# A two-layer encoder trunk on one core: Hyena pieces placed between the 24 gate and lift blocks of the attention branch, and 512-column products in the input and state-space stages

## Chip, core and metric

The kernel runs on one core of a Trainium2 chip (trn2). The metric is the device time in microseconds (us) of one execution. Engines: TensorE (PE, with its weight loads as PEld), VectorE (DVE), ScalarE (ACT), GpSimd (POOL) and SyncE (SP), which only issues DMAs. TensorE's clock has two levels, 1.2 and 2.4 GHz; a granted clock of 1.00 in a view is 2.4 GHz.

## The reference

Two layers, each of which projects the stream x (256 tokens, 2048 features), runs three mixers of width 1024 on it, lifts each mixer's output to 2048 features, gates and adds the three, and normalises. Cut to what matters:

```python
proj = x @ w_in[i]                       # inputs of the mixers, gate logits, ple logits
y_a = s5_mixer(a_x, ...) * silu(a_z)     # state space, per 16-channel group
filt_f = hyena_filters(L, ...)           # MLP -> taps (256, 2 dirs, 2 orders * 1024), rfft
y_b = hyena_mixer(b_u, ..., filt_f, ...) * silu(b_z)
y_c = mla_mixer(c_q, c_kv, c_kr, ...) * silu(c_z)
lifted = einsum('blnc,ncd->blnd', stack([y_a, y_b, y_c]), w_lift[i])
mixed = sum(sigmoid(gate_logits) * lifted, axis=branch) @ w_out[i]
x = layer_norm(ALPHA * x + mixed + ple)
# hyena_filters: h = sin-MLP(feats) @ w3 + b3; h *= decay; both directions joined;
#                divided by sum |h|; rfft
# hyena_mixer:   v, x1, x2 = split(short_conv3(u)); z = v
#                for n, gate in ((0, x1), (1, x2)):   # the two orders
#                    conv = irfft(rfft(z) * filt_f[:, n]); z = gate * (conv + bias[n] * z)
```

## The kernel before, in words

**Blocks.** The large weights come as 184 blocks per layer of 128x2048 float32, in halves of 128x1024, through a ring of four slots that SyncE fills in a fixed order. 170 of them are split into two parts: ACT copies a quarter (128x512) into WH in fp32r (L359, `make_wh`), DVE subtracts to get WL (L373, and L364 in the state-space loop; `make_wl`). WH and WL hold one block, in quarters of their own: a quarter of the next block can be written when PE has used that quarter of the current one (`parts_used`). The stream is split the same way into XH and XL. A tile product then takes three matmuls of 256 columns, `WH*XH`, `WH*XL`, `WL*XH` (L1354, `half_block`), so a block of 16 tiles takes 48.

**Stages of a layer**, in PE's order: `ax` (8 blocks, the S5 inputs, banks 0 and 1, evicted by ACT); `s5` (a loop of 8 turns, `ct`, with 8 blocks each, which project all else that is needed and whose results ACT evicts into PROJ, and between them the state-space work of one channel tile: `turn` L1390, `inputs` L1405, `lags` L1423, `outputs` L1440 and L1446); GLU and latent attention with unsplit weights (L1336, L1514); `lifta`, the 8 heads with the 24 gate and lift blocks of branch A between their parts; `filt`, the Hyena filters in four chunks of 512 channels (taps L1579 and L1580, their transform L1596, sums of absolute values L1603); `hy`, the two orders of the long convolution (transposes L1619, forward transform L1631, inverse L1639); `lift`, 24 blocks for branch B and 24 for branch C, in loops of 12; then `ple`, `out`, normalisation.

In `filt` and `hy` each step of PE is followed by one of DVE or ACT: DVE multiplies taps by DEC, which a POOL DMA brings (L874), forms ED and the sums (L884 to L889) and the short convolutions (L862 to L865); ACT takes absolute values and evicts (L1237 to L1248); DVE multiplies spectra (L920 to L928) and closes each order (L936 to L946). No weight block is used from the end of `lifta` to the first block of `lift`.

**What sets the order.** Each engine runs its own program in order; semaphores join them. `take_bank` waits until a PSUM bank has been read out, by counts that the table FILLS gives per stage.

Of the kernel before, what the change touches and what calls it, by code (L numbers as in the profile page):

```python
# [34 lines left out]
P = 128  # L35
# [59 lines left out]
STAGES = ["ax", "s5", "glu", "mla", "lifta", "filt", "hy", "lift", "ple", "out"]  # L95
# [83 lines left out]
def trunk(nc, x, blocks, lp, bc, w1, w2, b3, decay, feats, pT, pos, consts, out):  # L179
    with ExitStack() as ctx:  # L180
# [7 lines left out]
        XH, XL = sb("XH", DT * T, dt=F32R), sb("XL", DT * T, dt=F32R)  # L188
# [35 lines left out]
        xh, xl = split(XH[:], DT), split(XL[:], DT)  # L224
# [43 lines left out]
        HH, AB, ED, DEC, B3 = area(35, 8), area(121, 8), area(65, 8), area(25, 4), area(29, 2)  # L268
        FRE, FIM = area(89, 16), area(105, 16)
        ZT, YRE, YIM, TM = HH, ED, area(25, 8), AB  # L270
# [4 lines left out]
        YCH, YCL, YBH, YBL = parts("YCH", 89, 8), parts("YCL", 97, 8), parts("YBH", 105, 8), parts("YBL", 113, 8)  # L275
        MIXA = area(25, 16)
        MIX, PLE = area(73, 16), area(24, 16)
# [25 lines left out]
        b3_loaded, b3_cleared = sem("b3_loaded"), sem("b3_cleared")  # L303
        x_ready = sem("x_ready")
# [3 lines left out]
        us_written, us_landed, u4_loaded = sem("us_written"), sem("us_landed"), sem("u4_loaded")  # L308
        e_ready, bk_ready, bk_used = sem("e_ready"), sem("bk_ready"), sem("bk_used")
# [8 lines left out]
        sums_ready, sums_used = sem("sums_ready"), sem("sums_used")  # L318
        z_in, yf_ready, yb_ready = sem("z_in"), sem("yf_ready"), sem("yb_ready")
        mix_moved = sem("mix_moved")  # L320
# [15 lines left out]
        def split_number(layer, block_, turn=0, per=0):  # L336

            skipped = 0 if block_ <= B_LIFT0 else UNSPLIT[0] if block_ < B_W3 else UNSPLIT[1] if block_ <= B_OUT0 else UNSPLIT[2]
            return layer * SPLITS + (block_ - skipped + 1) + turn * per

# [55 lines left out]
        def _(pool):  # L396
# [5 lines left out]
            with pool.Fori(0, DEPTH) as layer:  # L402
# [32 lines left out]
                pool.wait_ge(mix_moved, layer + 1)  # L435
                for c in range(CHUNKS):
                    if c:

                        pool.wait_ge(psum_free[5], read_out(layer, "filt", 5, c - 1))
# [5 lines left out]
                    pool.dma_start(DEC, decay[c]).then_inc(b3_loaded, 16)  # L445
# [22 lines left out]
        def _(dve):  # L468
# [10 lines left out]
            with dve.Fori(0, DEPTH) as layer:  # L479
# [17 lines left out]

                make_wl(dve, v, layer, B_AX)
# [39 lines left out]
                st.did(v.reciprocal(S[1], S[0])); st.wait()  # L538
                make_wl(dve, v, layer, B_AX + 2)
# [12 lines left out]
                st.did(v.reciprocal(S[4], S[4])); st.wait()  # L552
                make_wl(dve, v, layer, B_AX + 3)
# [7 lines left out]
                st.did(v.tensor_tensor(S[6], S[6], S[4], ALU.mult)); st.wait()  # L561
                make_wl(dve, v, layer, B_AX + 4)
# [9 lines left out]
                st.did(v.tensor_tensor(lr[2], PA[:, 0:COLS], PB[:, 0:COLS], ALU.subtract)); st.wait()  # L572
                make_wl(dve, v, layer, B_AX + 5)
# [15 lines left out]
                product(square, powers(1, 2), powers(3, 2), 2, PA[:, 0:2 * COLS], PB[:, 0:2 * COLS])  # L589
                make_wl(dve, v, layer, B_AX + 6)  # L590
# [3 lines left out]
                product(factor, powers(0, 5), graw, 5, V[:, 0:5 * COLS], V[:, 2 * T:2 * T + 5 * COLS])  # L594
                make_wl(dve, v, layer, B_AX + 7)
# [18 lines left out]
                st.wait()  # L614
                make_wl(dve, v, layer, B_AX + 8)

                with dve.Fori(0, WT) as ct:
                    st.enter(ct, DVE_S5_STEPS)
                    wl_for = lambda j, q: make_wl_quarter(q, layer, B_S5 + j + 1, ct, 8)
# [44 lines left out]
                    wl_for(1, 1)  # L664
                    st.wait()
# [16 lines left out]
                    wl_for(2, 2)  # L682
                    st.did(v.tensor_tensor(terms(T2, 5), ci, g_r, ALU.mult))
# [6 lines left out]
                    wl_for(3, 2)  # L690
                    wl_for(3, 3)
# [9 lines left out]
                    wl_for(4, 1)  # L701
                    full(3, "s5", ct)
# [12 lines left out]
                    wl_for(5, 1)  # L715

# [14 lines left out]
                    wl_for(6, 1)  # L731
                    st.wait()
# [9 lines left out]
                    wl_for(7, 0)  # L742
                    st.did(v.tensor_tensor(split(V[:, 0:T], PAIRS), split(U4[:, bass.ds(ct * T, T)], PAIRS),
# [3 lines left out]
                    dve.wait_ge(y4_free, layer * WT + (ct + 1))  # L747
                    st.wait()
# [56 lines left out]
                for i in range(2):  # L805
# [6 lines left out]
                    round_phase(dve, st, *ARG, arg_ready)  # L812


                for h in range(HEADS):
# [23 lines left out]
                    if h < HEADS - 1:  # L839
                        make_wl(dve, v, layer, lift_a(3 * h + 3))  # L840
                    for b in range(2):
                        out_of(b, "lifta", h)
                        full(2 + b, "lifta", h)
                        free(v.tensor_tensor(split(MIXA, DT)[:, 2 * h + b, :], GA[:, b, :], bank[2 + b][:, 0:T], ALU.mult), 2 + b)
# [4 lines left out]
                dve.wait_ge(mix_moved, layer + 1)  # L849
                v.memset(B3, 0.0).then_inc(b3_cleared, 1)  # L850
# [4 lines left out]
                bct = tiles(BC, 0, 24)  # L855

                def short_conv(m):
                    u, o = PROJt[:, m, :], bct[:, m, :]
                    if m:

                        dve.wait_ge(z_in, layer * ZIN + m)
# [5 lines left out]


                hh = HH.rearrange("p (q c) -> p q c", q=4)
                for c in range(CHUNKS):  # L870
                    dve.wait_ge(b3_loaded, layer * (48 * CHUNKS) + (c + 1) * 48)
                    for q in range(4):
                        full(2 + q, "filt", c)
                        free(v.tensor_tensor(hh[:, q, :], bank[2 + q][:, :], DEC[:, (q % 2) * CW:(q % 2 + 1) * CW], ALU.mult), 2 + q)  # L874
                    for q in range(4):
                        out_of(2 + q, "filt", c)

                    v.memset(hh[0:1, 2, :], 0.0).then_inc(taps_ready, 1)
                    dve.wait_ge(taps_ready, layer * CHUNKS + (c + 1))
                    if c:  # L880

                        full(1, "filt", 2 * c - 1)
# [4 lines left out]
                    dve.wait_ge(abs_ready, layer * CHUNKS + (c + 1))  # L887
                    st.did(v.tensor_tensor(AB[:, 0:2 * CW], AB[:, 0:2 * CW], AB[:, 2 * CW:4 * CW], ALU.add)); st.wait()
                    v.tensor_tensor(AB[:, 0:CW], AB[:, 0:CW], AB[:, CW:2 * CW], ALU.add).then_inc(sums_ready, 1)  # L889
                    for m in range(6 * c, 6 * c + 6):  # L890
                        short_conv(m)
                    dve.wait_ge(ed_ready, layer * CHUNKS + (c + 1))
                dve.wait_ge(z_in, layer * ZIN + 24)
                full(6, "filt", 0)
                ns = NS
# [955 lines left out]
```

## Time and profile before

| | |
|---|---|
| median of 3 runs | 2981.0 us (2979.93 to 2981.59) |
| the profiled execution | 2978.65 us, of which 2977.0 us span |
| PE busy | 2751.8 us (92%), 20392 matmuls |
| DVE, ACT busy | 1846.7 us (62%), 1305.6 us (44%) |
| mean granted TensorE clock | 0.966 |

A busy time is the union of an engine's instructions; matmuls overlap each other, so their own durations add up to more than the time they take. The spacing of their starts is what one costs.

### The profile page before, as it was taken

The page shows a single profiled execution, that of the slowest core. Times are in us where ns is not written, and L with a number is a line of the kernel's source. Part 1 is how long each engine was busy: PE and PEld are TensorE (multiplying, and loading weights), DVE is VectorE, ACT ScalarE, POOL GpSimd, SP SyncE. Part 2 cuts the span into 40 slices and gives each one's busy share as a digit, 9 for nine tenths or more (in the row PEclk, how much of TensorE's full clock was granted, in tenths as well). Part 3 has the DMA queues.
Part 4 walks back from the last instruction along what each step waited for, and adds up shares of the span by engine and source line. Part 5 has one row for each costly group of instructions (what it writes and reads, how often), then busy time and mean ns, then how long its engine had stood idle before and what let it go on. Part 6 is the DMA issues. An engine that isn't in the chain of part 4 may idle for free.

```text
span 2977.0 us, 54930 instructions
## 1 busy us (share of the span) xinstructions
PE 2751.8 (92%) x20392; PEld 2570.1 (86%) x20392; DVE 1846.7 (62%) x3164; ACT 1305.6 (44%) x2319; POOL 109.1 (4%) x202
## 2 busy tenths in 40 slices
PE   6999999899977899999879999998999688999996
PEld 6999999779944799999779999997799447999986
DVE  6777767525567655565487777774355666555655
ACT  4455555525521244453335555555255212444532
POOL 1100000000000000000021000000000000000000
PEclk9999999899988999999989999999999889999999
DMA  6444444334421155555354444443344102555542
GB/s 226 151 146 144 144 144 141 103 128 157 149 64 36 68 180 181 183 177 171 106 177 148 147 142 148 138 145 102 136 149 142 57 29 86 180 183 180 178 165 92
DMA packets 115086, 411.08 MB, mean 138 GB/s; under 512 B 15300, under 2 KB 15322, under 8 KB 114448
## 3 DMA queue, kind: packets, MB, share of 16 engines
q1 hardware_dynamic: 106704, 390.12, 38.9%
q0 software_dynamic: 8256, 19.26, 2.1%
q8 instruction: 82, 1.34, 0.2%
q14 instruction: 44, 0.36, 0.0%
HBM read 403.02 MB, written 6.29 MB: 137 GB/s over the span
## 4 chain that ended last, share of the span: by engine, by line
PE 86%; DVE 7%; issue 3%; DMA 2%; ACT 2%; POOL 0%; DVEq 0%; PEldq 0%; POOLq 0%; ACTq 0%; PEld 0%; SPq 0%
PE bank L1354 64%; PE bank L1336 5%; PE bank L1446 2%; PE bank L1423 2%; PE bank L1405 2%; PE bank L1631 2%; PE bank L1639 1%; PE bank L1596 1%; PE bank L1390 1%; PE bank L1440 1%; PE bank L1514 1%; DMA ARENA<-in_decay 1%; PE bank L1579 1%; PE bank L1539 1%; PE bank L1538 1%
## 5 line engine op out<-in xcount | busy, mean ns | idle before, releaser
L359 ACT ACTIVATE WH<-ring 128x512 fp32r<-128x512 f32 x1360 | 856.4, 631 | 1107.1 <-PE bank L1354 982.3
L1354 PE MATMUL bank<-XH,WH 128*128 128x256 f32 x4160 | 1197.5, 288 | 75.2 <-DVE XL L501 44.6
L1354 PE MATMUL bank<-XL,WH 128*128 128x256 f32 x4160 | 1183.5, 284 | 0.0
L1354 PE MATMUL bank<-XH,WL 128*128 128x256 f32 x4160 | 1182.9, 284 | 0.0
L373 DVE TENSOR_TENSOR WL<-ring,WH 128x512 fp32r<-128x512 f32 x848 | 579.2, 691 | 512.8 <-ACT WH L359 507.9
L1354 PEld LDWEIGHTS bank<-XH,WH 128*128 128x128 f32 x4160 | 804.8, 193 | 84.9 <-DVE XL L501 45.0
L1354 PEld LDWEIGHTS bank<-XL,WH 128*128 128x128 f32 x4160 | 805.0, 194 | 0.1
L1354 PEld LDWEIGHTS bank<-XH,WL 128*128 128x128 f32 x4160 | 804.4, 193 | 0.0
L364 DVE TENSOR_TENSOR WL<-ring,WH 128x512 fp32r<-128x512 f32 x512 | 351.0, 688 | 192.3 <-ACT WH L359 186.2
L1336 PE MATMUL bank<-ARENA,ring 128*128 128x256 f32 x704 | 158.9, 388 | 20.2 <-ACT ARENA L1186 17.5
L1336 PEld LDWEIGHTS bank<-ARENA,ring 128*128 128x128 f32 x704 | 134.8, 194 | 43.6 <-issue 22.9
L1354 PE MATMUL bank<-MIXH,WH 128*128 128x256 f32 x512 | 144.5, 282 | 7.0 <-issue 5.5
L1354 PE MATMUL bank<-MIXL,WH 128*128 128x256 f32 x512 | 143.7, 281 | 0.0
L1354 PE MATMUL bank<-MIXH,WL 128*128 128x256 f32 x512 | 143.7, 281 | 0.0
L1354 PEld LDWEIGHTS bank<-MIXH,WH 128*128 128x128 f32 x512 | 96.5, 188 | 9.0 <-issue 6.7
L1354 PEld LDWEIGHTS bank<-MIXL,WH 128*128 128x128 f32 x512 | 96.5, 189 | 0.0
L1354 PEld LDWEIGHTS bank<-MIXH,WL 128*128 128x128 f32 x512 | 96.5, 188 | 0.0
L1639 PE MATMUL bank<-CON,ARENA 128*128 128x256 f32 x256 | 65.0, 421 | 19.3 <-DVE ARENA L928 19.3
L1639 PEld LDWEIGHTS bank<-CON,ARENA 128*128 128x128 f32 x256 | 54.4, 214 | 31.6 <-issue 22.6
L1354 PE MATMUL bank<-YAH,WH 128*128 128x256 f32 x256 | 75.0, 293 | 0.0
L1579 PE MATMUL bank<-ring,ARENA 64*128 64x512 f32 x64 | 27.3, 886 | 50.8 <-DMA ARENA<-in_decay 50.8
L1354 PE MATMUL bank<-YAH,WL 128*128 128x256 f32 x256 | 71.9, 281 | 0.0
(290 smaller groups left out, 3558.3 us busy)
## 6 DMA issues: line engine op xcount, KB each, us to landing
ring<-in_blocks SPq DMA_DIRECT2D x736, 512.0 KB, 3.3
ARENA<-in_bc POOLq DMA_DIRECT2D x2, 2048.0 KB, 8.4
ARENA<-in_decay POOLq DMA_DIRECT2D x8, 512.0 KB, 3.6
ARENA<-in_x SPq DMA_DIRECT2D x1, 2048.0 KB, 9.1
u_scratch<-ARENA POOLq DMA_DIRECT2D x16, 128.0 KB, 3.3
ARENA<-u_scratch POOLq DMA_DIRECT2D x64, 32.0 KB, 3.3
y_scratch<-ARENA POOLq DMA_DIRECT2D x16, 128.0 KB, 2.0
ARENA<-y_scratch POOLq DMA_DIRECT2D x64, 32.0 KB, 2.8
```

Of the source, the lines that this page charges most:

```text
L359: nc.scalar.activation(wh[q], raw(which[0], q), ACT.Copy).then_inc(wh_ready[q], 1)
L364: nc.vector.tensor_tensor(wl[q], raw(which[0], q), wh[q].bitcast(F32), ALU.subtract).then_inc(w_used[slot(which[0], q // 2)], 1)
L373: vec.tensor_tensor(wl[q], raw(which[0], q), wh[q].bitcast(F32), ALU.subtract).then_inc(w_used[slot(which[0], half)], 1)
L1336: ins = mm(o, w[:, (w0 + i) * P:(w0 + i + 1) * P], rhs(i), start=i == 0, stop=i == k - 1)
L1354: ins = mm(o, w_, x_, start=start and i == 0 and n == 0, stop=stop and i == 7 and n == 2)
L1390: ins = nc.tensor.transpose(bank[b][:, i * P:(i + 1) * P], part_of(E, i % 2, i // 2, q, P), ident)
L1405: ins = mm(o, ET[:, q % 2 * CW + i * P:q % 2 * CW + (i + 1) * P], u4(q), start=True, stop=True)
L1423: ins = mm(bank[4 + d][:, q * P:(q + 1) * P], b, f, start=(r == 0), stop=(r == 1))
L1446: ins = mm(o, f, x_, start=False, stop=(d == 1 and r == 1))
L1579: mm(bank[2 + q][:, :], H2[rows, t * P:(t + 1) * P], w[rows, c * CW:(c + 1) * CW], start=True, stop=False)
L1631: ins = mm(bank[b][:, :], tab[:, t, m * P:(m + 1) * P], ZT[:, t * W + half * CW:t * W + (half + 1) * CW], start=(t == 0), stop=(t == 1))
L1639: ins = mm(bank[c % 2][:, 0:T], yft[r][:, m, c * P:(c + 1) * P], (idft_sin if r else idft_cos)[:, m, :], start=(k == 0), stop=(k == 3))
```

## The change

**512-column products.** XH and XL become the two halves of one tensor XX. In `ax` and `s5` a tile product is two matmuls: WH against XH and XL together (512 columns, into columns 0 to 255 and 256 to 511 of one bank), and WL against XH (256 columns, onto the first half). ACT copies out the second half, then DVE adds the first half to it and frees the bank (`add_input`, `add_block`), at one place for each block in DVE's order. `lifta`, `lift`, `ple` and `out` keep three matmuls.

**Hyena pieces.** Stages `filt` and `hy` are gone. The 24 blocks of branch C come next after `lifta`, written out, as stage `hyc`; before block k PE does a piece of the Hyena work by its place s in the order (k = 12 o + s): s 0 and 3 taps, 2 and 5 filter transform, 6 transposes, 7 two quarters of the forward transform, 8 and 9 a quarter each (and in 8 the sums), 10 and 11 half of the inverse each. Filters are made per order o, in half the space. The pieces use banks 4 to 7. DVE does its pieces between the two halves of `make_wl` of block k + 1 and behind them. The w3 block is copied out of the ring by DVE, DEC has a semaphore of its own and shares memory with YIM, and the sum of branch A is written at its final place, so that the copy L848 goes. Branch B's 24 blocks follow, in the loop.

```diff
-    "filt": [8, 8, 4, 4, 4, 4, 1, 0],
-    "hy":   [8, 8, 4, 4, 4, 4, 4, 4],
-    "lift": [16, 16, 16, 16, 0, 0, 0, 0],
+    "hyc":  [8, 8, 8, 8, 18, 18, 20, 18],
+    "lift": [8, 8, 8, 8, 0, 0, 0, 0],
...
+                    if c == 0:
+                        pool.wait_ge(psum_full[5], nth(layer, "mla", 5, 8))
+                    elif c == 2:
+                        pool.wait_ge(psum_free[7], read_out(layer, "hyc", 7, hyc(0, "inv", 1)))
+                    pool.sem_inc(dec_free, 1)
+                    pool.dma_start(DEC, decay[c]).then_inc(dec_loaded, 16)
...
+                    def add_block(j):
+                        tile_ = PROJ[:, bass.ds(ct * (8 * T) + j * T, T)]
+                        dve.wait_ge(moved, layer * (9 * WT) + (ct * WT + (j + WT + 1)))
+                        free(v.tensor_tensor(tile_, tile_, bank[j % 2][:, 0:T], ALU.add), j % 2)
...
-                v.tensor_copy(MIX, MIXA).then_inc(mix_moved, 1)
...
+                for k in range(24):                                     # DVE
+                    o, s_ = k // 12, k % 12
+                    make_wl(dve, v, layer, B_LIFT + 24 + k + 1, halves=(0,))
+                    if s_ in (0, 3):
+                        taps_out(o, s_ // 3)
...
+                    if s_ in (7, 8, 9):
+                        if s_ == 8:
+                            full(6, "hyc", hyc(o, "sums", 0, 6))
+                            free(v.reciprocal(NS[:, o * 8:o * 8 + 8], bank[6][:, 0:8]), 6)
+                        product(o, (0, 1, 1)[s_ - 7], (0, 0, 1)[s_ - 7])
+                    if s_ in (10, 11):
+                        for m in range((s_ - 10) * 4, (s_ - 10) * 4 + 4):
+                            unconv(o, m)
+                    if o == 0:
+                        for m in {1: (0,), 2: (1, 2), 4: (4, 5), 5: (6, 7), 6: (9, 10)}.get(s_, ()):
+                            short_conv(m)
+                    else:
+                        for m in {1: (17, 18), 2: (19, 20), 4: (21, 22), 5: (23,)}.get(s_, ()):
+                            short_conv(m)
+                    make_wl(dve, v, layer, B_LIFT + 24 + k + 1, halves=(1,))
+                    if s_ in (0, 3):
+                        even_odd(o, s_ // 3)
+                    if s_ in (1, 4):
+                        sums(o, s_ // 3)
+                    if s_ == 7:
+                        product(o, 0, 1)
+                    if o == 0:
+                        for m in {2: (3,), 5: (8,), 6: (11,), 8: (12,), 9: (13, 14, 15), 11: (16,)}.get(s_, ()):
+                            short_conv(m)
+                    if k % 3 == 2:
+                        mix_in(k // 3, "hyc", k // 3)
...
-                        free(a.activation(PROJ[:, bass.ds(ct * (8 * T) + j * T, T)], bank[j % 2][:, 0:T], ACT.Copy), j % 2)
+                        a.activation(PROJ[:, bass.ds(ct * (8 * T) + j * T, T)], bank[j % 2][:, T:2 * T], ACT.Copy).then_inc(moved, 1)
...
+                        h, l = (buf[q][:, i % 4 * P:(i % 4 + 1) * P] for buf in (wh, wl))
+                        k = half * 8 + i
+                        ins = mm(bank[b][:, :], h, xx[:, :, k, :], start=(k == 0), stop=(k == DT - 1), skip_group_check=True)
+                        release(ins)
+                        ins = mm(bank[b][:, 0:T], l, xh[:, k, :], start=False, stop=(k == DT - 1), skip_group_check=True)
...
+                for k in range(24):                                     # PE
+                    o, s_ = k // 12, k % 12
+                    if s_ in (0, 3):
+                        taps(o, s_ // 3)
+                    if s_ in (2, 5):
+                        filter_dft(o, s_ // 3)
+                    if s_ == 6:
+                        turn_z(o)
+                    if s_ == 7:
+                        forward(o, 0, 0)
+                        forward(o, 0, 1)
+                    if s_ in (8, 9):
+                        forward(o, 1, s_ - 8)
+                    if s_ == 8:
+                        tap_sums(o)
+                    if s_ in (10, 11):
+                        inverse(o, s_ - 10)
+                    lift_blocks("hyc", k // 3, k % 3, hi, lo, layer * 4 + 2 if k == 2 else None, B_LIFT + 24 + k)
```

The order of instructions, at three places. First DVE in a turn of the `s5` loop, at the place of `frac_ready` (the WL row is the second quarter of block 2). Before:

```order
L661 TENSOR_TENSOR ARENA<-ARENA,CON 128x512
L163 REGISTER_ALU
L663 TENSOR_SCALAR ARENA<-ARENA 128x512
L364 TENSOR_TENSOR WL<-ring,WH 128x512
L163 REGISTER_ALU
L666 TENSOR_TENSOR ARENA<-ARENA 128x512
```

and of the changed kernel:

```order
L695 TENSOR_TENSOR ARENA<-ARENA,CON 128x512
L161 REGISTER_ALU
L697 TENSOR_SCALAR ARENA<-ARENA 128x512
L371 TENSOR_TENSOR WL<-ring,WH 128x512
L650 ISA
L651 ISA
L651 TENSOR_TENSOR ARENA<-ARENA,bank 128x256
L161 REGISTER_ALU
L701 TENSOR_TENSOR ARENA<-ARENA 128x512
```

An addition that reads a bank (L651) stands behind the WL quarter; it frees bank 0 for PE's block 2.

Second PE, between the last forward products of an order and the inverse ones. Before:

```order
L1631 MATMUL bank<-ARENA,CON 128x512 x4
L1303 REGISTER_ALU
L1631 MATMUL bank<-ARENA,CON 128x512 x2
L1303 REGISTER_ALU
L1631 MATMUL bank<-ARENA,CON 128x512 x2
L1303 REGISTER_ALU
L1639 MATMUL bank<-CON,ARENA 128x256 x8
```

and of the changed kernel, where block k = 8 ends (YCH, YCL are branch C's two parts) and s = 9 begins:

```order
L1447 MATMUL bank<-YCL,WH 128x256
L1447 MATMUL bank<-YCH,WL 128x256
L1396 REGISTER_ALU
L1746 MATMUL bank<-ARENA,CON 128x512 x2
L1396 REGISTER_ALU
L1746 MATMUL bank<-ARENA,CON 128x512 x2
L1396 REGISTER_ALU
L1447 MATMUL bank<-XX,WH 128x256 x2
L1447 MATMUL bank<-XX,WL 128x256
```

A quarter of the forward transform now stands between two blocks, and all of block 9 between it and the inverse (L1759).

Third DVE at the same place. Before, the product of spectra is followed by the next one or by the close of the order:

```order
L923 TENSOR_TENSOR ARENA<-bank,ARENA 128x512
L163 REGISTER_ALU
L925 TENSOR_TENSOR ARENA<-ARENA 128x512
L482 REGISTER_ALU x2
L928 TENSOR_TENSOR ARENA<-ARENA 128x512
L929 REGISTER_ALU
L936 TENSOR_SCALAR ARENA<-ARENA,PAR 128x256
```

and of the changed kernel:

```order
L380 TENSOR_TENSOR WL<-ring,WH 128x512 x2
L494 REGISTER_ALU
L954 TENSOR_TENSOR ARENA<-bank,ARENA 128x512
L955 TENSOR_TENSOR ARENA<-bank,ARENA 128x512
L956 TENSOR_TENSOR ARENA<-bank,ARENA 128x512
L957 TENSOR_TENSOR ARENA<-bank,ARENA 128x512
L161 REGISTER_ALU
L959 TENSOR_TENSOR ARENA<-ARENA 128x512
L495 REGISTER_ALU
L961 TENSOR_TENSOR ARENA<-ARENA 128x512
L962 REGISTER_ALU
L380 TENSOR_TENSOR WL<-ring,WH 128x512 x2
```

The product moved to between the first and the second half of WL of block 10.

## Rows read from the trace of the kernel before

**Rows 1.** The page: span, and the chain's shares by engine.

```profile
span 2977.0 us, 54930 instructions
...
PE 86%; DVE 7%; issue 3%; DMA 2%; ACT 2%; POOL 0%; DVEq 0%; PEldq 0%; POOLq 0%; ACTq 0%; PEld 0%; SPq 0%
```

**Rows 2.** Windows: stretch, length, busy PE, PEld, DVE, ACT, POOL, clock, DMA.

```profile
24.00:96.00 72.00, 64.53 (x486) 63.76 (x487) 58.61 (x143) 31.08 (x56) 22.00 (x40) 0.93 0.58 192
216.60:276.90 60.30, 60.30 (x516) 60.30 (x514) 44.20 (x68) 32.56 (x67) 2.76 (x5) 1.00 0.43 144
841.60:1015.00 173.40, 126.63 (x432) 76.99 (x432) 125.44 (x224) 28.23 (x35) 6.75 (x13) 0.87 0.08 26
```

**Rows 3.** The chain in order of time: start, length, what.

```profile
264.65 11.57 PE bank L1354 x96
276.21 0.87 PE bank L1390 x8
277.09 5.75 PE bank L1354 x48
...
324.88 11.57 PE bank L1354 x96
...
835.88 5.71 PE bank L1354 x48
...
1080.35 68.84 PE bank L1354 x576
...
1289.25 6.14 PE bank L1354 x49
```

**Rows 4.** Timeline of PE: merged runs of matmuls, in s5, mla, filt, hy.

```profile
245.88 1.83 PE L1423 MATMUL bank<-ARENA 128*128 128x128 f32 x15
...
263.59 1.06 PE L1446 MATMUL bank<-ARENA 128*128 128x64 f32 x8
...
598.72 49.59 PE L1336 MATMUL bank<-ARENA,ring 128*128 128x256 f32 x229
...
879.70 1.23 PE L1579 MATMUL bank<-ring,ARENA 64*128 64x512 f32 x4 [2.32 <-DMA ARENA<-in_decay]
...
883.43 7.13 PE L1596 MATMUL bank<-ARENA,CON 128*128 128x512 f32 x16
...
970.10 14.00 PE L1631 MATMUL bank<-ARENA,CON 128*128 128x512 f32 x32 [0.87 <-ACT ARENA L1248]
988.96 16.25 PE L1639 MATMUL bank<-CON,ARENA 128*128 128x256 f32 x62 [4.86 <-DVE ARENA L928]
```

**Rows 5.** Timeline of DVE in a turn of s5, and in ax.

```profile
273.25 1.29 DVE L364 TENSOR_TENSOR WL<-ring,WH 128x512 fp32r<-128x512 f32 x2
...
275.52 0.69 DVE L364 TENSOR_TENSOR WL<-ring,WH 128x512 fp32r<-128x512 f32 x1
...
81.02 2.50 DVE L373 TENSOR_TENSOR WL<-ring,WH 128x512 fp32r<-128x512 f32 x4
```

**Rows 6.** Timeline of ACT and DVE in filt, hy and lift.

```profile
863.00 0.41 DVE L862 TENSOR_SCALAR ARENA<-ARENA,PAR 128x256 f32<-128x256 f32 x1
...
864.48 0.41 DVE L862 TENSOR_SCALAR ARENA<-ARENA,PAR 128x256 f32<-128x256 f32 x1
...
973.99 0.69 DVE L920 TENSOR_TENSOR ARENA<-bank,ARENA 128x512 f32<-128x512 f32 x1 [7.37 <-PE bank L1631]
...
977.71 0.69 DVE L920 TENSOR_TENSOR ARENA<-bank,ARENA 128x512 f32<-128x512 f32 x1
...
1002.31 0.35 DVE L936 TENSOR_SCALAR ARENA<-ARENA,PAR 128x256 f32<-128x256 f32 x1
...
1004.14 0.35 DVE L936 TENSOR_SCALAR ARENA<-ARENA,PAR 128x256 f32<-128x256 f32 x1
...
1007.79 1.92 ACT L1251 ACTIVATE YBH<-ARENA 128x2048 fp32r<-128x2048 f32 x1 [37.92 <-DVE ARENA L946]
...
1084.29 0.69 DVE L373 TENSOR_TENSOR WL<-ring,WH 128x512 fp32r<-128x512 f32 x1 [0.73 <-ACT WH L359]
```

More of the change, by code:

```diff
@@ L92 @@
 SPLITS = BLOCKS - UNSPLIT[2]
-STAGES = ["ax", "s5", "glu", "mla", "lifta", "filt", "hy", "lift", "ple", "out"]
+STAGES = ["ax", "s5", "glu", "mla", "lifta", "hyc", "lift", "ple", "out"]
 FILLS = {
@@ L664, in _ @@
                     wl_for(1, 1)
+                    add_block(0)
                     st.wait()
@@ L1577, in filter_taps @@
                         rows = slice(64 * d, 64 * d + 64)
[L1578 to L1590 removed]
+                        take_bank(4 + q, "hyc", hyc(o, "taps", c, 4 + q))
@@ new lines, in taps, with tap_sums @@
+                        release(mm(bank[4 + q][:, :], H2[rows, t * P:(t + 1) * P], W3S[rows, (o * 2 + c) * CW:(o * 2 + c + 1) * CW], start=True, stop=False))
+                        done(mm(bank[4 + q][:, :], ones[rows, :], B3[rows, :], start=False, stop=True), 4 + q)
+                def tap_sums(o):
+                    pe.wait_ge(sums_ready, layer * CHUNKS + (o * 2 + 2))
+                    take_bank(6, "hyc", hyc(o, "sums", 0, 6))
+                    for j in range(8):
+                        ins = mm(bank[6][:, j:j + 1], SUM[:, j * P:(j + 1) * P], ones[:, 0:1], start=True, stop=True)
+                        if j < 7:
+                            release(ins)
+                    done(ins, 6)
@@ new lines, in filter_dft, with turn_z @@
+                        done(ins, 4 + q)
+                def turn_z(o):
+                    pe.wait_ge(z_in, layer * ZIN + (32 if o else 8))
+                    for q in range(4):
+                        t, half = q // 2, q % 2
+                        take_bank(4 + q, "hyc", hyc(o, "turn", 0, 4 + q))
+                        for j in range(4):
+                            ins = nc.tensor.transpose(bank[4 + q][:, j * P:(j + 1) * P], bct[:, half * 4 + j, t * P:(t + 1) * P], ident)
+                            if j < 3:
+                                release(ins)
+                        done(ins, 4 + q)
@@ new lines, in inverse, with lift_blocks @@
+                        done(ins, b)
+                def lift_blocks(stage, n, b, hi, lo, first, *which):
+                    if b < 2:
+                        take_bank(b, stage, n)
+                        whole_block(b, xh, xl, *which)
+                        return
+                    if first is not None:
+                        pe.wait_ge(yl_ready, first)
+                    for i in range(2):
+                        take_bank(2 + i, stage, n)
+                        done(half_block(bank[2 + i][:, 0:T], i, hi, lo, True, True, *which), 2 + i)
@@ L1664, in _ @@
+                hi, lo = split(YBH, WT), split(YBL, WT)
+                settle()
+                with pe.Fori(0, 2) as turn:
+                    for j in range(12):
+                        lift_blocks("lift", j // 3 + turn * 4, j % 3, hi, lo, layer * 4 + 3 if j == 2 else None, B_LIFT + 48 + j, turn, 12)
+                    settle()
                 for m in range(10):
```

411 lines of the change are left out of this document (214 added, 197 removed).

## The prediction

> **What bounds the kernel now.** I read the page first, then windows, one for each stage, then the chain in order of time, and only where it left PE the timelines. The chain that ends last is PE for 86% [rows 1], so what counts is PE's own time and the places where it waits. The windows split these. A turn of the `s5` loop takes 60.3 us with PE busy for all of it, the clock at 1.00 and DVE busy 44.2 [rows 2]; the chain there is blocks of 5.75 us (48 matmuls) with the state-space work between them, and two blocks from turn to turn lie 60.23 apart (264.65 to 324.88) [rows 3]. `ax` is mixed: 64.5 of 72 us [rows 2]. From 841.6 to 1015.0, `filt` and `hy`, PE is busy for 126.6 of 173.4 us, its clock is 0.87 on average, and the DMA engines are nearly idle (0.08) [rows 2]: each piece waits for DVE, ACT or DEC's transfer. So the two halves of the change touch different things: one shortens full PE time, the other fills idle PE time.
>
> **The wide products, per tile.** The spacing of matmul starts is the cost. In a block it is 120 ns for 256 columns (68.84 us for 576, with the few ns lost at block ends) [rows 3]. The float32 matmuls are two instructions each, and their spacings tell what is columns and what is not: 229 with 256 columns take 49.59 less a tail of 0.38, so 216 ns each; 15 with 128 columns (1.83 less 0.275) 111 ns; 8 with 64 columns (1.06 less 0.275) 112 ns [rows 4]. Half the columns did not make the last one cheaper, so some 112 ns is a floor that does not come from columns: every matmul has a weight load. In 216 ns that floor is hidden. The fp32r product with 256 columns, 107 ns of columns at 2.4 GHz, lies just above the floor, at 120. A wide tile is then one 512-column product, which I take at 216 ns as the float32 row with as many cycles, and one 256-column product, 120: 336 instead of 360, a gain of 24 ns. Bounds: if the 13 ns above the columns go with each matmul whatever its length, 226 + 120 = 346, a gain of 14; if the short one falls to the floor, 216 + 112, a gain of 32. Nearest to a long product whose weight load is covered is the 216 row, so 24.
>
> The Trainium skill (TensorE: Matmul & The Clock Gate, sections "Back-to-back issue gap" and "LDWEIGHTS") gives a gap of N/2.4 + 2.5 ns and a weight load of 128/1.2 = 107 ns, which would hide behind 256 columns; by it three products cost 328 and the wide pair 325 ns, so it would gain 3 ns a tile. The rows at 120 and 112 ns stand above its 109, so I go by the rows and keep its result as a rival.
>
> `s5`: 2 layers x 64 blocks x 16 tiles x 24 ns = **49.2 us less**.
>
> **Who then waits in s5.** DVE gets 8 additions of 256 columns per turn; an operation of DVE with 256 columns takes 0.41 us [rows 6], so 3.3 us, and DVE would be busy 47.5 of some 57.5. What matters is when they free a bank. `add_block(0)` stands behind the WL quarter that ran 275.52 to 276.13 [rows 5]; block 2, which needs bank 0, started at 277.09 on the chain, behind `turn` [rows 3]. Two shorter blocks bring that to 276.35. DVE before it ran without a gap (WL at 273.25, then 275.52) [rows 5], paced by arithmetic and not by PE, so the addition ends at 275.9 to 276.5 with its waits and signal: PE waits 0 to 0.5 us a turn; I take 0.4, 16 turns: **6.4 us more**. The other seven stand 1 us or more ahead of their bank's next use, and ACT's copies keep their length.
>
> **ax.** PE waits in it for 7.5 us as it is, and its last WL is made at 81.02, after DVE's scalar chain and memsets [rows 5]; that chain now has 8 additions in it. Earlier blocks wait there, so the 8 x 0.38 us per layer do not arrive, and some 2 x 0.5 us are added: **2 us more** in all (range: 3 us less to 6 more).
>
> **The Hyena pieces, PE's side.** At full clock, per layer: taps 4 x 3.7 (883.43 - 879.70) = 14.9; filter transform 4 x 16 x 0.43 = 27.9; forward 2 x 32 x 0.43 = 27.6; inverse 2 x 64 x 0.216 = 27.7 [rows 4]; transposes 2 x 16 x 0.109 (0.87 us for 8 [rows 3]) = 3.5; sums 2 x 16 x 0.112 = 3.6, at the floor. Together 105.2 us. Now this and both groups of 24 blocks run from 841.6 (835.88 + 5.71) to 1289.25, 447.7 us [rows 3]. After: 105.2, the first 24 blocks written out 24 x 5.75 = 138.0, the second group as now: three loops of 12 lie between 1080.35 and 1289.25, 69.6 each, so 139.3 [rows 3]. Sum 382.5, without any wait. So 65 us of waits and slow clock per layer can go; the question is what new waits come.
>
> **The new waits.** WH and WL hold one block, so DVE's order ties everything. In block k, started at B, the second WL quarter of block k+1 is done at B + 4.55 (1084.29 + 0.61 against 1080.35 [rows 3, 6]). Then comes a piece of length a, and only then the third quarter, needed by PE at B + 5.75 + H + 2.88, H being PE's own piece ahead of block k+1. So a piece may last up to 3.5 + H. DVE's pieces, from starts of like instructions: short convolution 1.48, product of spectra 3.72, close of an order 1.83 per tile in the second order, some 1.4 in the first (one instruction less) [rows 6]. Of the 173.4 us of `filt` and `hy` DVE was busy 125.4 [rows 2], and a WL of four quarters takes some 2.9 more in each 5.75 of a block: 125.4 + 24 x 2.9 = 195 of 243 us, so DVE is not the bound in total. Place by place:
> - s 6: transposes need convolutions 6 and 7, which stand behind the WL half of the block before: 4.55 + 2.96 - 5.75 = 1.8, first order only.
> - s 8: sums take bank 6 after the product started at 4.55 + 3.72 + 1.2 (two WL quarters) has read it, at 10.8; PE is there at 5.75 + 3.45: 1.6, twice.
> - s 10: the inverse needs the last product, 4.55 + 3.72 - 5.75 = 2.5, twice.
> - k 12: taps need the banks of the last closes, the third at 8.2 against 6.6: 1.7.
> - k 23: four closes, a = 7.3, while H = 0 for the block behind: 7.3 + 0.7 - 4.1 = 3.9. Then ACT's copy to YBH (1.92 [rows 6]) and DVE's YBL stand ahead of the next weights: some 2.2.
> - small ones (ZT, taps at s 3): 0.7.
>
> Sum 1.8 + 3.2 + 5.0 + 1.7 + 6.1 + 0.7 = 18.5 per layer. DEC of chunk 2 starts after the last close, and DVE asks for it behind PE's taps, which do not need it, so I cost it at nothing; before, such a transfer held PE's taps up by 2.32 us [rows 4], which it costs if DVE is late. The copy L848, B3's memset and DEC's wait all lie inside the 65. The gain is 447.7 - 382.5 - 18.5 = 46.7 per layer, **93.4 us less**.
>
> **Sum**, against the profiled execution: 2978.65 - 49.2 + 6.4 + 2 - 93.4 = 2844.5. The median of the runs is 2.35 above that execution: **2847 us**.
>
> **Rivals.**
> - *No gain in a wide tile*: 3 ns instead of 24, so 43 us less is gained: 2890. For it: a page's formula; against it: three spacings in the rows.
> - *DVE late among the blocks*: my waits assume that each piece starts on its mark. If lateness is handed on from block to block, every second block loses 1.5 us more, 18 to 30 us per layer: 2883 to 2907. For it: the pieces a = 3.72 at s 9, and taps at s 0 (by estimate 4 operations of 0.69 and their gaps), are at the limit of 3.5 where H is small. Against: H is 6.9 behind most.
> - *Slower*: fp32r with 512 columns runs at the float32 pace, 429 ns for 512 columns [rows 4] instead of 216. Then a tile costs 549, 2304 tiles (ax too) lose 0.19 us each, 435 us: about 3330. It decides from 277 ns for the long product, where 2304 x 37 ns eat the other 85. Against it: 256 columns take 120, not 216, and nothing in the rows makes the length of a product change its pace per column.
> - *Fewer waits than reckoned*: pieces hidden in H, tile at the floor: 2815 to 2825.
>
> **How the numbers follow.** My forecast 0.70 (its own range 2825 to 2875: tile 14 to 32 ns is +20 and -16, waits 10 to 30 per layer are -17 and +23), no gain in a tile 0.07, DVE late 0.13, fewer waits 0.06, slower 0.03, the rest 0.01 nothing measurable. The range over them, 2815 to 2892, leaves out the slower case, and some of the late one. 0.2% (6 us) is about what a measurement of this kernel can tell from no change. Faster 0.96, same 0.01, slower 0.03.
>
> **What would show it.** Spacings of 216 and 120 ns in alternation in `s5`; turns of some 57.5 us with a short wait of PE for DVE's addition ahead of block 2; `ax` no shorter; the clock at 1.00 from `lifta` to `ple` but for the end of `hyc`; that stage and the next together 401 us; PE's idle time at s 8, s 10 and at the change from `hyc` to `lift`, named after DVE. Wrong it would be with PE waiting for WL inside many blocks, with wide tiles at 360 ns, or with additions that hold up more than one block per turn.

## The result, and the profile after

The changed kernel takes 2878.2 us (median of 4, 2877.76 to 2883.01) against 2981.3 for the one before (median of 4): 103 us less, a ratio of 0.966 (95% interval 0.964 to 0.967). The forecast was 2847, in a range of 2815 to 2892: the way and most of the mechanisms held, and the gain was 103 us instead of 134. Two of the four executions of the run `hyena_only` below were disturbed (3451.74 and 6915.63 us) and are left out, so it has no interval.

The page of the profile, with the span and the chain's shares by engine, answers to [rows 1]:

```profile
span 2876.2 us, 50752 instructions
...
PE 87%; DVE 6%; issue 3%; ACT 2%; DMA 1%; DVEq 0%; PEldq 0%; POOLq 0%; POOL 0%; ACTq 0%; PEld 0%; SPq 0%
```

PE is as much the bound as before. The windows, in the columns of [rows 2], give a time for each stage: `ax` of layer 0 in full, a turn of `s5`, the first 173.5 us behind `lifta`, and `hyc` and `lift` together, up to `ple`:

```profile
25.16:100.32 75.16, 63.30 (x321) 53.96 (x322) 60.00 (x149) 30.34 (x54) 22.10 (x40) 0.91 0.55 178
218.05:276.85 58.80, 58.80 (x386) 53.17 (x385) 46.57 (x76) 32.49 (x65) 2.76 (x5) 1.00 0.44 146
838.50:1012.00 173.50, 167.47 (x1042) 135.79 (x1041) 130.50 (x235) 59.63 (x99) 4.63 (x9) 0.99 0.34 115
838.50:1243.72 405.22, 390.14 (x2691) 343.09 (x2690) 268.64 (x472) 152.10 (x256) 5.18 (x10) 0.99 0.39 132
```

The third row is the stretch that followed `lifta` in [rows 2] too: PE was busy for 126.63 of 173.40 us at a clock of 0.87, and is now for 167.47 of 173.50 at 0.99. The same stretches before, as far as [rows 2] don't have them:

```profile
24.43:95.37 70.94, 63.90 (x481) 63.13 (x481) 57.55 (x141) 30.33 (x54) 21.44 (x39) 0.93 0.58 189
1499.91:1572.58 72.67, 64.88 (x481) 64.30 (x481) 57.67 (x141) 28.79 (x52) 21.60 (x39) 0.89 0.56 185
```

That makes a budget. `hyc` and `lift`: 447.7 to 405.2 in layer 0, 449.5 to 405.3 in layer 1, **86.7 less**. `s5`: 60.23 to 58.82 a turn, 16 turns, **22.6 less**. `ax`: 70.94 to 75.16 and 72.67 to 73.91 in layer 1, **5.5 more**. These are 103.8, and the span fell by 100.8. The 3 us between are in stages that the change does not touch: 3.8 us more from the GLU to the first attention head (the clock in the latent projections of layer 0 reads 0.92 instead of 1.00), 0.7 and 1.1 us more ahead of the two `ax`, and 2.9 us less in the last sums of the normalisation of layer 0, where the clock reads 1.00 instead of 0.71.

Here is how a wide tile looks in PE's timeline (start, length, what), at the beginning of a block of `s5`:

```profile
266.01 0.40 PE L1475 MATMUL bank<-XX,WH 128*128 128x512 f32 x1
266.24 0.28 PE L1477 MATMUL bank<-XX,WL 128*128 128x256 f32 x1
266.36 0.39 PE L1475 MATMUL bank<-XX,WH 128*128 128x512 f32 x1
266.59 0.27 PE L1477 MATMUL bank<-XX,WL 128*128 128x256 f32 x1
266.70 0.40 PE L1475 MATMUL bank<-XX,WH 128*128 128x512 f32 x1
```

From wide start to wide start it is 0.35 and 0.34 us. Over all 2304 tiles the medians are 231 ns from the wide product to the short one and 117 from there to the next wide one: 348 ns a tile, against 360 before and 336 forecast.

The list of what PE waited for (line <- what, us in total, times, longest) shows the new waits of `hyc`. L1759 (inverse), L1711 (sums) and L1734 (transposes) wait for DVE, as forecast, and L1475 <- L515 is the addition in `ax`:

```profile
PE bank L1475 <- DVE ARENA L515: 14.8, 2, 7.4
...
PE bank L1759 <- DVE ARENA L961: 9.5, 4, 2.4
PE bank L1447 <- DVE WL L380: 8.2, 6, 2.8
...
PE bank L1711 <- DVE ARENA L955: 4.9, 4, 1.2
PE bank L1734 <- DVE ARENA L913: 3.6, 4, 1.7
```

### The profile page after: what moved, and what is told of

Its sections match the earlier page's. It is cut to its first block, busy times and chain, and to the rows that moved or that the text cites. A ratio compares the mean times of both kernels' runs of the same rounds, so it can differ in the third digit from the quotient of the medians.

```text
span 2876.2 us, 50752 instructions
## 1 busy us (share of the span) xinstructions
PE 2709.4 (94%) x18088; PEld 2429.8 (84%) x18088; DVE 1876.5 (65%) x3312; ACT 1297.3 (45%) x2319; POOL 108.7 (4%) x202
## 3 DMA queue, kind: packets, MB, share of 16 engines
q8 instruction: 86, 1.41, 0.2%
## 4 chain that ended last, share of the span: by engine, by line
PE 87%; DVE 6%; issue 3%; ACT 2%; DMA 1%; DVEq 0%; PEldq 0%; POOLq 0%; POOL 0%; ACTq 0%; PEld 0%; SPq 0%
PE bank L1447 36%; PE bank L1475 18%; PE bank L1477 9%; PE bank L1429 5%; PE bank L1568 2%; PE bank L1545 2%; PE bank L1759 2%; PE bank L1527 2%; PE bank L1723 2%; PE bank L1746 1%; PE bank L1512 1%; PE bank L1562 1%; PE bank L1636 1%; DVE WL L380 1%; PE bank L1661 1%
## 5 line engine op out<-in xcount | busy, mean ns | idle before, releaser
L1475 PE MATMUL bank<-XX,WH 128*128 128x512 f32 x2304 | 826.1, 402 | 69.3 <-DVE XX L520 46.5
L1447 PE MATMUL bank<-XX,WH 128*128 128x256 f32 x3712 | 683.3, 286 | 12.6 <-DVE WL L380 8.2
L1477 PE MATMUL bank<-XX,WL 128*128 128x256 f32 x2304 | 646.6, 281 | 0.0
L1447 PEld LDWEIGHTS bank<-XX,WH 128*128 128x128 f32 x3712 | 581.0, 192 | 30.7 <-issue 23.9
L1475 PEld LDWEIGHTS bank<-XX,WH 128*128 128x128 f32 x2304 | 438.0, 190 | 171.8 <-DVE XX L520 46.9
L1447 PE MATMUL bank<-XX,WL 128*128 128x256 f32 x1856 | 526.3, 284 | 0.0
L1477 PEld LDWEIGHTS bank<-XX,WL 128*128 128x128 f32 x2304 | 439.8, 191 | 0.0
L1447 PEld LDWEIGHTS bank<-XX,WL 128*128 128x128 f32 x1856 | 357.2, 192 | 0.0
L1447 PE MATMUL bank<-YCH,WH 128*128 128x256 f32 x256 | 79.1, 309 | 0.0
L1447 PE MATMUL bank<-YCL,WH 128*128 128x256 f32 x256 | 74.7, 292 | 0.0
```

The lines of the kernel that those rows point to most:

```text
L1447: ins = mm(o, w_, x_, start=start and i == 0 and n == 0, stop=stop and i == 7 and n == 2)
L1475: ins = mm(bank[b][:, :], h, xx[:, :, k, :], start=(k == 0), stop=(k == DT - 1), skip_group_check=True)
L1477: ins = mm(bank[b][:, 0:T], l, xh[:, k, :], start=False, stop=(k == DT - 1), skip_group_check=True)
```

## Experiments

Each run stands beside runs of the kernel before on the same chip (medians 2978.8 to 2981.7).

**The halves apart.** `wide_only` is the kernel before with the 512-column products; `hyena_only` the changed one with

```diff
-                    wide_block(m % 2, B_AX + m)
+                    whole_block(m % 2, xh, xl, B_AX + m)
-                        wide_block(j % 2, B_S5 + j, ct, 8)
+                        whole_block(j % 2, xh, xl, B_S5 + j, ct, 8)
```

and ACT's evictions as before. 

> The kernel before with the 512-column products alone (ax and s5), the Hyena stages as they were. Theory A (the parts add up; the changed kernel's trace has a turn of s5 at 58.8 instead of 60.2 us, 16 turns, and ax later by some 3 us a layer): 2981 - 22 + 5 = 2964 us, 2958 to 2970. Rival (a wide tile gains 24 ns as forecast, and s5 in the changed kernel is slowed by something of the Hyena half, such as what lies where in SBUF): turns of 57.5 us, about 2941 us. Spacings under A: 231 and 117 ns.

 

> The changed kernel with three 256-column products in ax and s5, evicted by ACT alone as before: the Hyena half alone. Theory A (parts add up, Hyena half worth 42.5 us a layer): 2981 - 85 = 2896 us, 2890 to 2900. Rival (the 93 us of the forecast, with an interaction that takes some back when both are made): 2888 us or less.

`wide_only` took 2967.05 us (0.9952, 0.9936 to 0.9969), 14.6 less. `hyena_only` took 2893.41 and 2895.71, some 87 less. 14.6 + 87 = 102 of the 103: the halves add up. The miss of the forecast lies in each by itself, not between them. The turns of `s5` are 58.8 us in the first and 60.23 in the second.

The Hyena half was not taken apart further, and a rival explanation of part of its gain stands untested. The longest wait of PE in the old `filt` is for DEC's transfer, in the list of waits of the kernel before:

```profile
PE bank L1579 <- DMA ARENA<-in_decay: 50.8, 8, 9.1
```

That is 25 us of the 65 that could go in each layer. PE's taps don't read DEC; they wait for it because its transfer raises the same semaphore as that of B3, which they do read. The change gives DEC a semaphore of its own, and in the changed kernel no wait of PE is put down to this transfer. How much of the 86.7 us this alone would have given, with `filt` and `hy` left where they were, no run shows: DVE needs DEC right behind the taps, so some of the wait would have come back one step later.

**`ax` with three products** (`narrow_ax`: the first of those two edits alone). 

> The changed kernel with three products in ax alone, wide ones kept in s5. Theory A (the additions in DVE's scalar chain make ax late, by 4.9 us in layer 0 and 1.1 to 2.4 in layer 1): 2878 - 6 = 2872 us. Rival (ax ends later for another reason, such as the clock at its start, or the shorter matmuls): 2878 us or more, since the wide tiles gain up to 3 us there.

2871.14 us (0.9630, 0.9614 to 0.9646), 7 us less than the changed kernel. Why is in the chain of the changed kernel, in order of time:

```profile
84.13 1.82 DVE WL L380 x3
85.96 0.34 DVE ARENA L515
86.30 0.44 issue
86.74 0.79 PE bank L1475
87.53 0.21 PE bank L1477
87.75 0.43 PE bank L1475
88.17 0.21 PE bank L1477
```

The addition L515 stands behind WL, which stands behind the memsets. PE waits 7.4 us for it, once in each layer (the list of waits above), and the tiles behind the wait then start every 0.64 us instead of 0.35. The window of those tiles has a granted clock of 0.50, 1.2 GHz, after the pause:

```profile
86.74:91.60 4.86, 4.86 (x15) 4.19 (x16) 1.99 (x4) 0.63 (x1) 2.76 (x5) 0.50 0.65 223
```

With narrow products `ax` takes 70.29 us:

```profile
24.80:95.09 70.29, 62.74 (x448) 60.28 (x449) 57.23 (x141) 30.32 (x54) 21.43 (x39) 0.95 0.58 188
```

PE pauses at the same place there too, for 4.2 us and for WL alone, and the tiles behind that pause are 0.64 us apart as well:

```profile
81.57 0.70 DVE WL L380
82.32 0.50 PE bank L1467
```

So the pause and the lower clock behind it are not new; what the additions brought is that it is 3.2 us longer, and that PE starts again at 86.74 instead of 82.32. Two things make these 4.4 us, as DVE's timeline in the changed kernel shows:

```profile
83.13 0.42 DVE L515 TENSOR_TENSOR ARENA<-ARENA,bank 128x256 f32<-128x256 f32 x1
83.47 2.49 DVE L380 TENSOR_TENSOR WL<-ring,WH 128x512 fp32r<-128x512 f32 x4
85.88 0.41 DVE L515 TENSOR_TENSOR ARENA<-ARENA,bank 128x256 f32<-128x256 f32 x1
```

DVE's chain is 1.9 us later: the first quarter of WL is done at 84.16, where `narrow_ax` has it at 82.27. And PE does not start then, but at 86.74. Ahead of the loop's first block its program waits until both banks of `ax` have been read out, though that block writes bank 0 alone. Bank 0 is free with the addition of 83.13; the one that frees bank 1, at 85.88, stands behind all four quarters of WL. So in a stage that DVE's chain paces, the trade of PE time for a DVE addition did not pay as it was placed here. With that addition ahead of WL, or PE's wait for bank 1 behind its first block, up to 2.5 us a layer of it could come back by estimate (86.74 less 84.16); neither was tried.

**Why 348 and not 336.** `contig` stores the two parts tile by tile, so that the 512 columns lie in one piece:

```diff
-        XH, XL = XX[:, 0:DT * T], XX[:, DT * T:2 * DT * T]
+        xpart = XX[:].rearrange("p (k r t) -> p k r t", r=2, k=DT)
+        XH, XL = xpart[:, :, 0, :], xpart[:, :, 1, :]
```

> The changed kernel with the two parts of the stream interleaved by tile, so that the 512 columns of a wide product lie in one piece of memory instead of two. Theory B (the 231 ns come from reading two pieces): the spacing falls to some 216, a tile to 333 ns, 2048 tiles x 15 ns = 31 us less, 2847 us. Theory C (fp32r products pay some 13 to 18 ns over their columns wherever the data lie): 231 stays, 2878 us; some us more are possible where DVE and ACT write with gaps between the pieces.

2881.15 us (0.9665, 0.9648 to 0.9683), spacings 231 and 117: the place of the data has no part in the spacing. Three more change the products themselves, in the changed kernel:

```diff
-                        ins = mm(bank[b][:, :], h, xx[:, :, k, :], ...)
-                        ins = mm(bank[b][:, 0:T], l, xh[:, k, :], ...)
   # sizes:
+                        ins = mm(bank[b][:, 128:512], h, xx[:, :, k, 64:256], ...)
+                        ins = mm(bank[b][:, 0:P], l, xh[:, k, 0:P], ...)
   # bf16 (the wide one alone):
+                        ins = mm(bank[b][:, :], h.bitcast(BF)[:, 1::2], xx[:, :, k, :].bitcast(BF)[:, :, 1::2], ...)
   # wl512 (the one of WL alone):
+                        ins = mm(bank[b][:, :], l, xx[:, :, k, :], ...)
```

> The changed kernel with shorter products in ax and s5: the wide one has 384 columns, the one of WL 128; a quarter of the input columns is left out of each tile. Theory C1 (what a product costs over its columns grows with them: 0.434 ns a column and 9 ns, the line through 231 and 120): 176 ns, and the short one at the floor, 112. Theory C2 (13 to 18 ns for each product whatever its length, between 120 and 231): 173 to 178, which can't be told from C1; but the short one then stands at 112 by the floor and not at 53 + 13. Rival (the 112 is no floor for fp32r, 128 columns cost 53 + 13 = 66 ns behind a long product whose time hides the weight load): 66 ns, and 2048 tiles x 106 ns = 217 us less than 2878; by the floor 2048 x (348 - 288) = 123 us less, 2755.

 

> The changed kernel with the wide product alone in bfloat16, read from the high halves of the same words (both operands lose their lower 16 bits; the product of WL stays in fp32r). Theory D (the 231 ns are fp32r's own): some 215 ns, as a pass of float32 with 512 columns costs (429 / 2), so 2048 tiles x 16 ns = 33 us less, 2845. Theory E (any product of 512 columns among weight loads costs 231 ns): no change, 2878.

 

> The changed kernel with the product of WL too over all 512 columns in ax and s5 (the term WL*XL is added to the other half; nothing is left out). Theory C2 (a product costs its columns at 2.4 GHz and some 14 ns, whatever its length): a tile 2 x 227 = 454 ns, 106 more, and 2048 tiles of s5 x 106 = 217 us, plus 20 to 25 in ax: 3118 us. Theory C1 (0.434 ns a column and 9 ns): 2 x 231 = 462, 3135 us. Theory F (the loss is in the change between products of unlike length, two of 512 columns run at 216): 432 ns, 84 more, 3070 us.

`sizes` leaves out a quarter of the input columns of each tile and `bf16` the lower 16 bits of both operands of the wide product; `wl512` adds the term WL*XL. One execution each: `sizes` 2799.66 us, `bf16` 2899.48, `wl512` 3109.66. First the timeline of PE in `wl512`, then in `sizes`, then in `bf16`:

```profile
169.05 0.40 PE L1475 MATMUL bank<-XX,WH 128*128 128x512 f32 x1
169.28 0.40 PE L1477 MATMUL bank<-XX,WL 128*128 128x512 f32 x1
169.52 0.39 PE L1475 MATMUL bank<-XX,WH 128*128 128x512 f32 x1
```

```profile
139.59 0.39 PE L1475 MATMUL bank<-XX,WH 128*128 128x384 f32 x1
139.82 0.22 PE L1477 MATMUL bank<-XX,WL 128*128 128x128 f32 x1
139.88 0.39 PE L1475 MATMUL bank<-XX,WH 128*128 128x384 f32 x1
```

```profile
148.55 0.40 PE L1476 MATMUL bank<-XX,WH 128*128 128x512 bf16 x1
148.59 0.48 PE L1478 MATMUL bank<-XX,WL 128*128 128x256 f32 x1
148.91 0.40 PE L1476 MATMUL bank<-XX,WH 128*128 128x512 bf16 x1
```

In `wl512` all products are alike, so the spacing is the cost of one: median 227 ns both ways, where the columns take 213. A turn of `s5` takes 72.5 us, 13.7 more than 58.8: 107 ns for each of its 128 tiles, 454 in all. That is theory C2: the columns and 13.7 ns for each product, whatever its length (256 and 512 were measured). It gives 120 for 256 columns (before: 120), 227 + 120 = 347 for the wide pair (348), and 174 + 112 = 286 for `sizes` (medians 228 + 59 = 287), the short one at the floor of [rows 4].

`sizes` and `bf16` also show how the stamps mislead. The start of a short product stands 228 ns behind a wide one of 384 columns, and the next wide one 59 ns behind that; with bfloat16 it is 39 and 321. Neither is a cost; only the sum over the tile is, 287 and 360: the spacing of starts is what a product costs only where its neighbours are like it. So 231 and 117 are not the costs of 512 and 256 columns either, though I first took them for that (C1, which asked for 462 in `wl512`). The expectation that 59 would mean no floor fell by the same sum. In `bf16` the tile is 12 ns dearer than in fp32r, not cheaper; whether by the change of type inside the tile or by the reading of every second element was not separated.

`sizes` answers one more question: it saves 61 ns a tile, 7.8 us a turn, but its turns are 53.9, only 4.9 shorter. PE is idle there for 2 us a turn, and its chain goes over DVE's WL and additions:

```profile
149.31:203.27 53.96, 51.93 (x387) 51.05 (x386) 46.12 (x76) 32.25 (x65) 2.76 (x5) 1.00 0.47 161
```

```profile
157.57 0.60 DVE WL L371
158.17 0.34 DVE ARENA L651
158.56 0.44 PE bank L1475
```

By this, and as an estimate, most of a gain of 24 ns a tile, 3 us a turn, would have come; much more would not.

**DVE's place in line in `hyc`.** `products_first` puts each product of spectra where PE has its input ready and DVE is idle; `pieces_first` moves the closes and two convolutions too. The edit, with the part of `pieces_first` alone marked; the calls at their old places, which go, are not shown:

```diff
                 for k in range(24):
                     o, s_ = k // 12, k % 12
+                    if s_ == 7:
+                        product(o, 0, 0)
+                    if s_ == 8:
+                        full(6, "hyc", hyc(o, "sums", 0, 6))
+                        free(v.reciprocal(NS[:, o * 8:o * 8 + 8], bank[6][:, 0:8]), 6)
+                        product(o, 1, 0)
+                    if s_ in (10, 11):                              # pieces_first
+                        for m in range((s_ - 10) * 4, (s_ - 10) * 4 + 4):
+                            unconv(o, m)
+                    if k == 5:                                      # pieces_first
+                        for m in (6, 7):
+                            short_conv(m)
                     make_wl(dve, v, layer, B_LIFT + 24 + k + 1, halves=(0,))
...
+                    if s_ == 7:
+                        product(o, 0, 1)
...
                     make_wl(dve, v, layer, B_LIFT + 24 + k + 1, halves=(1,))
...
+                    if s_ == 8:
+                        product(o, 1, 1)
```

What it rests on is a pause of DVE in the changed kernel: its input from PE (banks 4 and 5) is ready near 908, but the product at 916.03 stands behind a WL that can't be made before block 7 runs:

```profile
908.26 0.48 DVE L913 SCALAR_TENSOR_TENSOR ARENA<-ARENA,PAR 128x255 f32<-128x255 f32 x1
913.86 0.69 DVE L380 TENSOR_TENSOR WL<-ring,WH 128x512 fp32r<-128x512 f32 x1 [5.12 <-ACT WH L366]
...
916.03 0.68 DVE L954 TENSOR_TENSOR ARENA<-bank,ARENA 128x512 f32<-128x512 f32 x1
```

> The changed kernel with DVE's products of spectra placed by when PE has them ready: the first one ahead of the first WL half of block 8 (DVE idles 5.1 us there), the second between the halves, the third behind the reciprocal and ahead of block 9's WL, the last behind block 9's WL. Theory A (the 1.8 us ahead of the sums, the 1.4 inside block 8 and the 2.6 ahead of the inverse, in each of four orders, are DVE's place in line and nothing else): 4 x 5.8 = 23 us less, 2855 us, 2850 to 2862. Rival (lateness is handed on, since the same DVE work moves ahead of WL and PE then waits for WL in blocks 8 to 10): 2878 us or slower.

 

> The same, and the closes of an order (s 10 and 11) and convolutions 6 and 7 ahead of the first WL half of the next block too. Theory A: beside the 23 us it takes away the 1.9 us ahead of the transposes, some 2 us ahead of the taps of k 12, and some 4 of the 6.1 us at the change to the loop, 8 us a layer: 2878 - 23 - 16 = 2839 us, 2832 to 2850. Rival (closes ahead of WL make WL late, as DVE now waits for PE's inverse one by one): as products_first or slower.

`products_first` took 2858.41 us (0.9595, 0.9579 to 0.9611), `pieces_first` 2837.65 (0.9527, 0.9511 to 0.9543): 20 and 40.6 us less than the changed kernel. The rival, that lateness is handed on, fell. In `pieces_first` the stage reads, in the columns of the windows:

```profile
836.98:1221.24 384.26, 381.56 (x2691) 338.18 (x2690) 268.66 (x472) 152.06 (x256) 5.18 (x10) 1.00 0.41 139
```

384.3 us, where my sum without any wait was 382.5, and 405.2 in the changed kernel: the sum 105.2 + 138.0 + 139.3 of the forecast is confirmed to 2 us. Of the 22.7 us that the changed kernel lost over it, 20.9 were the order of DVE's pieces, with what followed from it. The waits of PE for DVE that are left in the stage:

```profile
PE bank L1453 <- DVE WL L380: 1.7, 2, 0.9
...
PE bank L1740 <- DVE ARENA L913: 0.3, 2, 0.2
```

**Together.** `best` is `pieces_first` with three products in `ax`, `pieces_narrow` the same with three in `s5` too. 

> The kernel pieces_first with three products in ax (wide ones in s5 alone). The parts add up: 2837.65 less the 7 us that narrow products in ax gave before, 2831 us, 2827 to 2835. Rival (part of that was chance between chips): 2838.

 

> The kernel pieces_first with three products in ax and s5, ACT evicting alone. What do wide products in s5 give on their own: by a tile of 348 instead of 360 ns and the short wait for the addition, 22 us, so 2831 + 22 = 2853 us, 2848 to 2858. Rival (with the Hyena waits gone, nothing changes that value, but if the clock falls for the busier PE, the narrow kernel is hit less): under 2848.

`best` took 2829.36 us (0.9492, 0.9479 to 0.9505), the fastest that does the whole work, 49 us less than the changed kernel. `pieces_narrow` took 2849.44 (0.9560, 0.9546 to 0.9575): wide products in `s5` are worth 20 us, within the 22 of their turns.

## Why the prediction was right, and where it was off

Both halves gained, by the paths that were named, and PE's work in the Hyena stage came out to 2 us. The span fell by 33 us less than forecast: 24.6 are the wide tile, 6.7 the Hyena stage and 3.5 `ax`, 4.4 came back at the addition in `s5`, and 3 lie in stages that the change does not touch.

**The size of a wide tile** is the term of the sum that was mis-sized: forecast 24 ns a tile and 49.2 us, measured 12 ns and 24.6 us. The step that failed is "Nearest to a long product whose weight load is covered is the 216 row, so 24": a float32 instruction of 256 columns (a matmul is two of them) takes the time of 512 columns, 216 ns, but an fp32r product that has 512 costs 227. The bound that the prediction had written down and passed over, 13 ns above the columns for each product whatever its length, 346 ns, is what `wl512` showed. Why the float32 instruction pays only 3 ns over that stays open. The rival "no gain in a wide tile" was wrong as well: the Trainium skill (TensorE: Matmul & The Clock Gate, "Back-to-back issue gap") gives N/2.4 + 2.5 ns for a product by itself, without the load of its weights, which is 216 for 512 columns; here each product has a load, and the runs show 227. Of the 40 ns that three products pay over their columns one product's share goes, 13, not 2.5.

**The addition in `s5`**: forecast 0.4 us a turn. The start of block 2 stands 0.19 us behind the transposes instead of 0.03, and block 3 is up to 0.1 longer; 8 blocks x 0.19 = 1.54 less the measured 1.41 leaves 0.1 a turn, 2 us instead of 6.4. The mechanism and the place were right (DVE's L651 at 277.10, PE's next block at 277.71). The size was small because the tile gained less: with 24 ns a tile PE would have been there 0.4 us sooner, by estimate (2 blocks x 16 tiles x 12 ns).

**`ax`**: forecast 2 us more, range to 6; measured 5.5 in the stage, 7 by `narrow_ax`. The step that failed is "the 8 x 0.38 us per layer do not arrive, and some 2 x 0.5 us are added". PE's idle time in the two stages grew by 8.0 us (71.0 - 63.9 and 72.7 - 64.9 before, 75.2 - 63.3 and 73.9 - 62.9 now), against 2.6 less busy time: the additions do arrive, 1.9 us of them at the first quarter of WL for the loop, and the last of them holds PE by the bank that it frees, a wait that the sum did not have. The lower clock behind the pause is little of it, since it was there before: the stages read 0.93 and 0.89 then, 0.91 and 0.88 now.

**The Hyena stage**: forecast 401 us with its sum of 382.5 and waits of 18.5; measured 405.2 and 22.7. The two agree in part by luck: of the 405.2 us PE is idle for 15.1, less than forecast, and most of the rest is a lower clock behind three of the pauses, a term that the prediction put at nothing ("the clock at 1.00 from `lifta` to `ple` but for the end of `hyc`"). By place, in a layer, the spacing in the changed kernel less that in `pieces_first`: s 6, 1.9 (forecast 1.8); s 10, 2 x 2.6 (5.0); k 12, 2.2 (1.7); k 23, 5.2 (6.1); s 8, 2 x 3.2 (3.2). At k 23 the waits themselves were 3.2 us, half of the forecast, and the block between them ran at a clock of 0.66, which makes up 1.7 more. At s 8 the wait for bank 6 was there with its 1.6 us, but the block behind took 7.3 us instead of 5.8. The windows show why, from the pause through the sums into block 8:

```profile
917.37:922.29 4.92, 3.70 (x10) 1.44 (x9) 4.89 (x9) 0.90 (x2) 0.00 (x0) 1.00 0.34 112
922.29:924.10 1.81, 1.81 (x17) 1.81 (x17) 1.81 (x4) 0.00 (x0) 0.00 (x0) 1.00 0.87 269
924.10:926.52 2.42, 2.42 (x15) 2.42 (x14) 0.53 (x1) 0.00 (x0) 0.00 (x0) 0.57 0.00 0
926.52:931.40 4.88, 4.88 (x38) 4.88 (x38) 2.56 (x5) 1.89 (x3) 0.00 (x0) 0.86 0.00 0
```

Behind 1.22 us of idle time and sums of one column the granted clock reads 0.57 in the first 2.42 us of the block, which is mostly its lower level of 1.2 GHz, and 0.86 in the other 4.88; at the same place in the second order the first 2.35 us read 0.50. With the pause gone (`pieces_first`) that block runs at 1.00 in 5.78 us. So the wait there cost about twice its length. DEC's transfer held nobody, as forecast. But the prediction named only one of its waits before, 2.32 us, where the four of a layer add up to 25: the 65 us that could go were right, but not how large this part of them is. The sum's 27.9 for the filter transform is 27.5 by its own factors, too little to matter. The rivals "DVE late among the blocks" and "slower" did not come: PE waited for WL inside no block of the stage ahead of the change to the loop, and an fp32r product keeps its pace per column at 512.

## What to carry to other kernels

Price a matmul by its columns and a fixed part, and get the fixed part from a stretch in which all products are alike: merging products saves one fixed part each (here 13 ns of 360), not the difference to another type's pace. When idle-time work is put among full-time work, the sum of the work tells what can be had, and each piece's place in the slower engine's queue tells what is; put each where its input is ready and the engine pauses, which gave 41 us more here without removing an instruction. Before an eviction is split between two engines, ask in which stage the second one already sets the pace, and behind what the operation that frees the bank will stand. And look for who shares a semaphore: a wait named after a transfer can be one that its engine never needed.

## What the runs showed of the hardware

- An fp32r product with a weight load of its own costs 227 ns with 512 columns (`wl512`) and 120 with 256 (the kernel before), its columns at 2.4 GHz and 13.7 ns; a float32 instruction of 256 columns, of which a matmul has two, costs 216, twice its columns and 3 ns.
- A matmul's start stamp is not the start of its columns when neighbours differ in length or type: 39 and 321 ns for a pair that costs 360, 228 and 59 for one that costs 287.
- A bfloat16 product of 512 columns, read with a step of two elements between fp32r ones, made the tile 12 ns dearer (360 instead of 348).
- Behind a pause of 1.2 us and 16 one-column products the granted clock read 0.57 in the next 2.42 us, and 0.50 at the same place in the second order; without the pause it read 1.00.
